# Two transformer blocks on one core: buffers shifted by 128 bytes, the inverse's turns as products on own blocks, one scan, output stored tile by tile

## The chip, the core and the metric

The kernel runs as one program on 1 core of one Trainium2 chip. The metric is the time of one execution on the device, in microseconds (us). The engines are TensorE (PE; its weight loads are PEld), VectorE (DVE), ScalarE (ACT), GpSimd (POOL) and SyncE (SP), which here only issues DMAs. Each engine runs its own instructions strictly in program order; semaphores are the only links between engines.

## The reference

The input x has 512 tokens of 1024 features. The first block is attention (a sparse NSA branch and an MLA branch, gated and summed), then an MLP with 4096 hidden features and a squared relu. The second block is a mixer of two branches, then such an MLP again, then a final norm:

```python
def second_block(x, ...):
    h = _rmsnorm(x, norm_mix_g[l])
    proj = h @ w_in[l]                       # r, k, v (1024 each), GLU (2048), gates (2048)
    ...
    a_out = _rwkv7_mixer(h, r, k, v, ...)    # 16 heads of 64, see below
    c_out = _conformer_conv_mixer(glu_in, conv_w[l], ...)   # 31 taps over time, per feature
    merged = gates[:, :, 0] * (a_out @ w_rwkv_proj[l]) + gates[:, :, 1] * (c_out @ w_conv_proj[l])
    x = x + merged @ w_out[l]
    h2 = _rmsnorm(x, norm_ff_g[l])
    x = x + jnp.square(jax.nn.relu(h2 @ w_ff1[l])) @ w_ff2[l]
    return _rmsnorm(x, norm_final_g)

    # the recurrence in _rwkv7_mixer, per head, state S (64 x 64):
    # S_t = S_{t-1} diag(w_t) + (S_{t-1} (-kk_t)) (kk_t * a_t)^T + v_t k_t^T ;  o_t = S_t r_t
```

Everything is float32.

## The kernel before

**Layout.** Features lie on the 128 partitions, 8 tiles of 128 features (`KT`), and the 512 tokens along the free dimension. A big product (helper `three`, L765 to L767) takes its weights in two parts, `whi` and `wlo`, and its activations in two parts as well (`ah`, `oh`, `yh`, `coh`, `aoh`, `hidden`), all in the type fp32r: per 128 x 128 block of weights three matmuls of 512 columns, hi by hi, hi by lo, lo by hi. ACT makes `whi` (L1295) and POOL `wlo` (L680) from the weight block that SP has loaded into `raw`. Everything else on PE is plain fp32. In nearly all products the weights are stationary and the activations are the moving operand; in the product of `uv` (L768 to L770) `cqh` is stationary and `whi` moves.

**Buffers.** They lie in SBUF in the order in which they are declared. In the built program the start addresses within a partition are: `whi` 54016, `wlo` 62208, `ah` 70400, all multiples of 256. After the small `rs`, `mod` and `modg` the rest begins at 117888, which is 128 more than a multiple of 256: `oh`, `coh` and the first `hidden` are there, and `cqh`, `yh`, `aoh` and the second `hidden` at 150656, also 128 over. `x` is at 16512, 128 over as well, and `tmp` at 103168, a multiple of 256.

**Stages.** Attention and its output (to about 560 us), MLP 1 (to about 960), the mixer of block 2 with the loop described next (to about 1713), its projections `pr`, `pc`, `wo2` (to about 1870), MLP 2, and the final norm. An MLP takes the hidden features in 4 chunks of 1024; per chunk 8 products that read `ah` and 8 that read `hidden`.

**The mixer's loop.** `rwkv_order()` returns one list of named steps, and every engine walks it and issues its share: that list is each engine's order. It has 8 tiles j of two heads (`hh` 0 and 1), each in chunks of 64 tokens. The recurrence is solved chunk by chunk with products: `mb` and `mk` make the masked matrices (`ma`, `mr`, `ka`, `kr`), then a 64 x 64 triangular matrix is inverted in `LEVELS` = 5 doubling levels. A level `lv` is: `ip` (PE: `ma` by the turned inverse `ix`, L1167; DVE masks it out of PSUM, L2153), `iy` (PE: `ip` by `iy`, L1172; DVE adds it to the inverse `iy`, L2161), and, but for the last level, `inv` (PE turns `iy`, L1156; ACT copies it into `ix`, L1334). Each is done for both heads. `iy` and `ix` hold both 64 x 64 blocks of a 128-token tile with zeros beside them, so 128 columns for each of the 4 token tiles. The first level's `iy0` is made by DVE (head 0) and POOL (head 1). After the levels come `tav` (L1178), `rr` (L1184, DVE L2170), `opa` (L1202), `pt`, `qq`, six state steps `st` (PE L1226, DVE L2182 and L2185) one after another, and `ost`. `opv` (L1195) stands ahead of the levels.

**What fills the waits.** Between these dependent steps stands work of the next tile. `tile_ahead(j + 1)` lists it: parts of the r, k, v and GLU products (two 128 x 128 blocks, 6 matmuls, each) and the steps that hang on them (`scan`, a running sum of 64 tokens, eight of them, L2071; `mix`, L2026; `kk`, L2083 to L2088; `kkss`, L2093, ending in a reciprocal, L2095, that waits for ACT's square root). `slot(taps)` puts one part and its steps, and then `taps` taps of the 31-tap convolution, which are one DVE instruction each (L2005). There are 14 slots of 2 taps inside the levels, 2 of 1 tap behind `tav` and `rr`, and the last tap comes ahead of the next tile's convolution input (L2124). The products of ("glu", j + 1, 0) lie between the state steps as filler for PE, one block each; the last tile has no such product.

**PSUM.** Banks are handed out in turn by `bank_places`; PE waits for the bank's reader before it fills one again.

## Time and profile before

| | us |
|---|---|
| median of 3 runs (lowest, highest) | 2248.98 (2247.29, 2251.56) |
| the profiled execution, its own time | 2251.5 |
| its span, first to last instruction | 2249.7 |
| PE busy | 2103.1 (93% of the span) |
| DVE, ACT, POOL busy | 1188.6, 800.9, 736.3 |
| mean granted clock of TensorE | 0.971 of 2.4 GHz |

How to read the rows further down. A row of windows has: the stretch (us from the span's start), its length, busy us and instructions of PE, PEld, DVE, ACT and POOL, the granted clock of TensorE (1.00 is 2.4 GHz), the DMA engines' busy share, GB/s. A row of the timeline has: start (us), length (us), engine, line, operation, output and inputs, shape, how many instructions were merged, and in brackets how long the engine had been idle and what ended it. Matmuls are pipelined and their ends are modelled, so what one costs is read from start to start; a plain fp32 matmul is two instructions in the trace, a turn (`transpose`) one. A row of one tile's instructions has the count, the shortest, median and longest duration in ns, the first and last start in us, and shapes. A row of waits has the total us, how many, and the longest. DVE instructions that read two operands from SBUF while POOL works can take much longer than their median.

### The profile page before, as it was taken

Reading aid. Unit: us, or ns where it says so; the run is one execution under the profiler, and the core shown is the slowest. Engines: PE = TensorE matmul, PEld = TensorE weight load, DVE = VectorE, ACT = ScalarE, POOL = GpSimd, SP = SyncE. Lnnn points to the kernel's source line nnn. Section 1 sums busy time; section 2 is a strip of 40 time slices with the busy share of each in tenths; the row PEclk is TensorE's granted clock in tenths of the full one; section 3 lists DMA queues with packets and bytes.
Section 4 is the critical chain, followed back from the end, with each engine's and each line's share of the span. In section 5 each row is a group of like instructions: output and inputs, shape, how many; then the busy total and the mean of one; then the engine's idle time right before and its main releaser. Section 6 shows DMA issues by size and latency. Waiting matters only on the chain. (4 is left out here: it accounts for less than half of the span.)

```text
span 2249.7 us, 34219 instructions
## 1 busy us (share of the span) xinstructions
PE 2103.1 (93%) x13936; PEld 1650.2 (73%) x13936; DVE 1188.6 (53%) x1963; ACT 800.9 (36%) x1292; POOL 736.3 (33%) x347
## 2 busy tenths in 40 slices
PE   6898989999999999988999999999999998999997
PEld 5775567887788888766777776676777787888885
DVE  6427775333652342738778668777813456523322
ACT  2336655223332232443333333333333434322321
POOL 0221021444344444542232133223223443444442
PEclk9989999999899999999999999999999999999998
DMA  7531011533232333231101111101122322233331
GB/s 263 187 128 38 30 47 66 175 116 95 70 98 94 94 96 97 82 106 41 34 32 46 34 34 45 43 29 44 44 85 98 122 94 76 93 94 98 99 95 57
DMA packets 51450, 186.51 MB, mean 83 GB/s; under 512 B 5728, under 2 KB 6880, under 8 KB 50784
## 3 DMA queue, kind: packets, MB, share of 16 engines
q1 hardware_dynamic: 47520, 174.49, 23.8%
q10 hardware_dynamic: 3776, 9.83, 1.2%
q8 instruction: 113, 1.85, 0.4%
q14 instruction: 41, 0.34, 0.0%
HBM read 178.01 MB, written 6.29 MB: 82 GB/s over the span
## 5 line engine op out<-in xcount | busy, mean ns | idle before, releaser
L680 POOL TENSOR_TENSOR wlo<-raw,whi 128x1024 fp32r<-128x1024 f32 x266 | 644.5, 2424 | 1337.8 <-ACT whi L1295 1337.7
L765 PE MATMUL psum<-ah,whi 128*128 128x512 f32 x1288 | 538.2, 418 | 26.5 <-POOL wlo L680 16.0
L766 PE MATMUL psum<-ah,whi 128*128 128x512 f32 x1288 | 512.0, 398 | 0.0
L767 PE MATMUL psum<-ah,wlo 128*128 128x512 f32 x1288 | 511.6, 397 | 0.0
L1295 ACT ACTIVATE whi<-raw 128x1024 fp32r<-128x1024 f32 x266 | 280.2, 1054 | 367.2 <-PE psum L767 304.0
L765 PEld LDWEIGHTS psum<-ah,whi 128*128 128x128 f32 x1288 | 247.5, 192 | 98.2 <-POOL wlo L680 26.1
L767 PEld LDWEIGHTS psum<-ah,wlo 128*128 128x128 f32 x1288 | 247.2, 192 | 54.3
L766 PEld LDWEIGHTS psum<-ah,whi 128*128 128x128 f32 x1288 | 248.3, 193 | 43.5 <-issue 0.2
L2005 DVE SCALAR_TENSOR_TENSOR x<-upad,vec,x 128x512 f32<-128x512 f32 x240 | 211.5, 881 | 5.2
L765 PE MATMUL psum<-hidden,whi 128*128 128x512 f32 x536 | 213.0, 397 | 0.0
L766 PE MATMUL psum<-hidden,whi 128*128 128x512 f32 x536 | 212.7, 397 | 0.0
L767 PE MATMUL psum<-hidden,wlo 128*128 128x512 f32 x536 | 212.6, 397 | 0.0
L1716 DVE SCALAR_TENSOR_TENSOR hidden<-tmp,hidden 128x512 fp32r<-128x512 f32 x72 | 154.0, 2139 | 49.0 <-ACT hidden L1330 49.0
L765 PEld LDWEIGHTS psum<-hidden,whi 128*128 128x128 f32 x536 | 101.3, 189 | 24.5
L767 PEld LDWEIGHTS psum<-hidden,wlo 128*128 128x128 f32 x536 | 101.2, 189 | 24.5
L766 PEld LDWEIGHTS psum<-hidden,whi 128*128 128x128 f32 x536 | 101.2, 189 | 24.4
L1334 ACT ACTIVATE sq<-psum 128x512 f32<-128x512 f32 (+2 forms) x88 | 49.1, 572 | 195.9 <-PE psum L767 195.2
L1942 DVE TENSOR_TENSOR tmp<-sq 128x512 f32<-128x512 f32 x64 | 48.6, 759 | 105.6 <-ACT sq L1334 102.2
L1950 DVE TENSOR_TENSOR x<-psum,x 128x512 f32<-128x512 f32 x32 | 22.1, 692 | 142.2 <-PE psum L767 142.2
L1952 DVE SCALAR_TENSOR_TENSOR x<-psum,mod,x 128x512 f32<-128x512 f32 x32 | 24.0, 749 | 116.4 <-PE psum L767 116.3
L1334 ACT ACTIVATE ix<-psum 128x512 f32<-128x512 f32 x80 | 45.9, 597 | 75.4 <-PE psum L1156 74.6
L1427 ACT ACTIVATE sm<-sm,stat 128x128 f32<-128x128 f32 (+3 forms) x96 | 53.2, 555 | 42.4 <-DVE stat L1857 42.0
(340 smaller groups left out, 2916.8 us busy)
## 6 DMA issues: line engine op xcount, KB each, us to landing
raw<-in_w SPq DMA_DIRECT2D x322, 512.0 KB, 3.5
x<-in_x SPq DMA_DIRECT2D x1, 2048.0 KB, 7.9
x_kept<-x ACTq DMA_DIRECT2D x1, 2048.0 KB, 9.7
ao_kept<-ao ACTq DMA_DIRECT2D x8, 256.0 KB, 2.0
aof<-ao_kept ACTq DMA_DIRECT2D x1, 2048.0 KB, 10.8
x<-x_kept ACTq DMA_DIRECT2D x1, 2048.0 KB, 8.4
out<-x SPq DMA_DIRECT2D x1, 2048.0 KB, 6.3
lwt<-in_lw ACTq DMA_DIRECT2D x8, 128.0 KB, 2.0
```

Of the source, the lines that this page charges most:

```text
L680: pool.tensor_tensor(wlo[:, s % NHL, :], raw_of(SPLITS[s]), whi[:, s % NHL, :].bitcast(F32), ALU.subtract).then_inc(lo_done, 1)
L765: pe.matmul(dst, wh, h_, start=first, stop=False)
L766: pe.matmul(dst, wh, l_, start=False, stop=False)
L767: return pe.matmul(dst, wl, h_, start=False, stop=last)
L1295: act.activation(whi[:, s % NHL, :], raw_of(SPLITS[s]), ACT.Copy).then_inc(hi_done, 1)
L1334: emptied_by(act.activation(dst, bank(name) if src is None else src, kw.pop("func", ACT.Copy), **kw), name)
L1427: act.activation(probs[:, u % PROBS[tag], 0:w], probs[:, u % PROBS[tag], 0:w], ACT.Exp, bias=st[:, u % PROBS[tag], 0:1], scale=-1.0, accum ...
L1716: dve.scalar_tensor_tensor(dst_lo, tmp[:, n % NTMP, :], bias, dst_hi.bitcast(F32), ALU.add, ALU.subtract).then_inc(hl_ready, 1)
L1942: dve.tensor_tensor(slot(("hid", n, c, m)), sq[:, e % 2, :], sq[:, e % 2, :], ALU.mult).then_inc(pre_split, 1)
L1950: emptied_by(dve.tensor_tensor(x[:, m, :], bank(what), x[:, m, :], ALU.add), what)
L1952: emptied_by(dve.scalar_tensor_tensor(x[:, m, :], bank(what), gate(m), x[:, m, :], ALU.mult, ALU.add), what)
L2005: ins = dve.scalar_tensor_tensor(acc, src, tap, acc, ALU.mult, ALU.add)
```

## The change

- A buffer `to_line` of 128 bytes that nothing uses is declared behind `modg`. All buffers behind it that are not in the mixer loop's own group move up by 128 bytes: `oh`, `coh`, `hidden` to 118016, `cqh`, `yh`, `aoh`, `hidden` to 150784, all now multiples of 256. In the loop's group sizes change too, and `ma` to `st` go from multiples of 256 to 128 over.
- `ix` and `iy` hold only their own blocks, 64 columns for each token tile. `inv` turns each block by a product with a 64 x 64 part of the unit matrix (16 matmuls of 64 x 64 for two heads, where there were 8 turns of 128 x 128). The additions on DVE and POOL and ACT's copies have 256 columns instead of 512.
- `rr`, `opv` and `opa` do both heads in one step, head 0 and head 1 in turn for each token tile; `rr` needs one PSUM bank and one DVE instruction of 128 partitions instead of two of 64.
- The masking of `mr` and `kr` is one DVE instruction instead of four. The eight scans are one scan of 512 columns that multiplies its running sum by a mask (`later`, 512 more columns in `rw`) which is 0 at a chunk's start.
- The reciprocals behind ACT's square roots become steps of their own, `kkinv` and `gninv`, that stand later in the list.
- The taps are spread by a table `TAPS`, with 3 behind `qq` and one behind every second state step.
- The output is stored by 8 DMAs of 256 KB, each behind its own tile of the final norm, where one DMA of 2 MB was behind the last.

```diff
+TAPS = (1, 2, 2, 2, 2, 1, 2, 2, 2, 0, 2, 1, 1, 2, 2, 1)
...
-            + v[2:3] + [("lg2", j)] + v[3:] + [("kkss", j)] + g[:1] + [("mix", j, 2)] + g[1:2] + [("kkb", j)] + g[2:3] + [("bonus", j)]
+            + v[2:3] + [("lg2", j)] + v[3:] + [("kkss", j)] + g[:1] + [("mix", j, 2), ("kkinv", j)] + g[1:2] + [("kkb", j)] + g[2:3] + [("bonus", j)]
...
-        out += [("akv", j, 0), ("akv", j, 1), ("inv", j, 1, 0), ("opv", j, 0), ("opv", j, 1)]
+        out += [("akv", j, 0), ("akv", j, 1), ("inv", j, 1, 0), ("opv", j)]
+        if j:
+            out.append(("gninv", j - 1))
...
-        out += [("tav", j, 0), ("tav", j, 1)] + slot(1) + [("rr", j, 0), ("rr", j, 1)] + slot(1)
-        out += [("opa", j, 0), ("opa", j, 1)] + last[:1] + [("pt", j, 0), ("pt", j, 1)] + last[1:2] + [("qq", j, 0), ("qq", j, 1)]
+        out += [("tav", j, 0), ("tav", j, 1)] + slot() + [("rr", j)] + slot()
+        out += [("opa", j)] + last[:1] + [("pt", j, 0), ("pt", j, 1)] + last[1:2] + [("qq", j, 0), ("qq", j, 1), ("conv", j, 3)]
...
-            out += [("st", j, c)] + last[1 + c:2 + c]
+            out += [("st", j, c), ("conv", j, (c + 1) % 2)] + last[1 + c:2 + c]
...
+        sb("to_line", [P, 32])
...
-            ix, iy, ip = both("ix", TT * P), both("iy", TT * P), both("ip", TT * CH)
+            ix, iy, ip = both("ix", TT * CH), both("iy", TT * CH), both("ip", TT * CH)
...
-            sp.wait_ge(xn_ready, 2 * KT)
-            sp.dma_start(out.rearrange("p (k s) -> p k s", k=KT), x[:, :, :]).then_inc(stored, 16)
-            sp.wait_ge(stored, 16)
+            for k in range(KT):
+                sp.wait_ge(xn_ready, KT + k + 1)
+                sp.dma_start(out[:, k * S:k * S + S], x[:, k, :]).then_inc(stored, 16)
+            sp.wait_ge(stored, 16 * KT)
...
-                    for t in range(TT):
-                        mm = pe.transpose(b[:, t * P:t * P + P], iy[hh][:, t, :], eye)
+                    for t, own in own_chunks:
+                        dst, src = b[own, t * CH:t * CH + CH], iy[hh][own, t, :]
+                        mm = pe.matmul(dst, src, eye[own, own], start=True, stop=True)
...
-                    hh = f[2]
-                    wait_emptied(pe, ("tav", j, hh))
+                    for hh in range(2):
+                        wait_emptied(pe, ("tav", j, hh))
                     for t in range(TT):
-                        mm = pe.matmul(b[RN * hh:RN * hh + RN, t * P:t * P + P], tav[:, t, 0, hh, :], mr[hh][:, t, :],
-                                       start=True, stop=True)
+                        for hh in range(2):
+                            mm = pe.matmul(b[RN * hh:RN * hh + RN, t * P:t * P + P], tav[:, t, 0, hh, :], mr[hh][:, t, :],
+                                           start=True, stop=True)
...
-                    for c in range(NCK):
-                        cols = slice(c * CH, c * CH + CH)
-                        last = dve.tensor_tensor_scan(cw[:, cols], ones[:, 0:CH], sw[:, cols], 0.0, ALU.mult, ALU.add)
...
+                    last = dve.tensor_tensor_scan(cw[:, :], later, sw[:, :], 0.0, ALU.mult, ALU.add)
...
+                elif kind == "kkinv":
                     dve.wait_ge(kkroot_done, j + 1)
                     dve.reciprocal(nrt[:, :], nrt[:, :]).then_inc(nrm_ready, 1)
```

PE ahead of the levels of tile 6, before (in names of `order` rows the head is the last digit of a buffer; xN merges equal rows):

```order
L1156 MATMUL psum<-eye_ones,iy0 128x128 x4
L1243 MATMUL psum<-rw,sq 128x2 x4
L1162 MATMUL psum<-vtk,ka0 64x64 x8
L1162 MATMUL psum<-vtk,ka1 64x64 x8
L1156 MATMUL psum<-eye_ones,iy1 128x128 x4
L1195 MATMUL psum<-kr0,vtk 64x128 x4
L1195 MATMUL psum<-kr1,vtk 64x128 x4
L1167 MATMUL psum<-ix0,ma0 64x64 x8
```

The same place now:

```order
L1164 MATMUL psum<-eye_ones,iy0 64x64 x8
L1253 MATMUL psum<-rw,sq 128x2 x4
L1170 MATMUL psum<-vtk,ka0 64x64 x8
L1170 MATMUL psum<-vtk,ka1 64x64 x8
L1164 MATMUL psum<-eye_ones,iy1 64x64 x8
L1205 MATMUL psum<-kr0,vtk 64x128
L1205 MATMUL psum<-kr1,vtk 64x128
L1205 MATMUL psum<-kr0,vtk 64x128
L1205 MATMUL psum<-kr1,vtk 64x128
```

Four turns of 128 x 128 per head became eight products of 64 x 64, and the eight products of `opv` now change the head each time; the order of the steps is the same.

DVE around the scan, between the additions of level 2 and the masking of level 3 in a middle tile, before:

```order
L2161 TENSOR_TENSOR iy<-psum,iy 128x512 x2
L2005 SCALAR_TENSOR_TENSOR x<-upad,vec,x 128x512 x2
L2026 SCALAR_TENSOR_TENSOR rkv<-psum,omu,rkvp 128x512
L2071 SCALAR_TENSOR_TENSOR cw<-eye_ones,sw 128x64 x8
L2005 SCALAR_TENSOR_TENSOR x<-upad,vec,x 128x512 x2
L2153 TENSOR_TENSOR ip<-psum,rw 128x256 x2
```

Now:

```order
L2161 TENSOR_TENSOR iy<-psum,iy 128x256 x2
L2015 SCALAR_TENSOR_TENSOR x<-upad,vec,x 128x512 x2
L2036 SCALAR_TENSOR_TENSOR rkv<-psum,omu,rkvp 128x512
L2079 SCALAR_TENSOR_TENSOR cw<-rw,sw 128x512
L2015 SCALAR_TENSOR_TENSOR x<-upad,vec,x 128x512
L2153 TENSOR_TENSOR ip<-psum,rw 128x256 x2
```

One scan stands where eight were, and one tap is gone from behind it.

DVE from the masking of level 4 to that of level 5, before:

```order
L2153 TENSOR_TENSOR ip<-psum,rw 128x256 x2
L2026 SCALAR_TENSOR_TENSOR rkv<-psum,omu,rkvp 128x512
L2083 TENSOR_SCALAR kk<-rkv,vec 128x512
L2084 TENSOR_SCALAR tmp<-rate,vec 128x512
L2086 SCALAR_TENSOR_TENSOR rkv<-tmp,rkv 128x512
L2088 SCALAR_TENSOR_TENSOR tmp<-rkv,vec 128x512
L2005 SCALAR_TENSOR_TENSOR x<-upad,vec,x 128x512 x2
L2161 TENSOR_TENSOR iy<-psum,iy 128x512 x2
L2005 SCALAR_TENSOR_TENSOR x<-upad,vec,x 128x512 x2
L2093 TENSOR_SCALAR nrt<-psum 128x8
L2095 RECIPROCAL nrt<-nrt 128x8
L2005 SCALAR_TENSOR_TENSOR x<-upad,vec,x 128x512 x2
```

Now:

```order
L2153 TENSOR_TENSOR ip<-psum,rw 128x256 x2
L2036 SCALAR_TENSOR_TENSOR rkv<-psum,omu,rkvp 128x512
L2088 TENSOR_SCALAR kk<-rkv,vec 128x512
L2089 TENSOR_SCALAR tmp<-rate,vec 128x512
L2091 SCALAR_TENSOR_TENSOR rkv<-tmp,rkv 128x512
L2093 SCALAR_TENSOR_TENSOR tmp<-rkv,vec 128x512
L2161 TENSOR_TENSOR iy<-psum,iy 128x256 x2
L2015 SCALAR_TENSOR_TENSOR x<-upad,vec,x 128x512 x2
L2098 TENSOR_SCALAR nrt<-psum 128x8
L2015 SCALAR_TENSOR_TENSOR x<-upad,vec,x 128x512
L2153 TENSOR_TENSOR ip<-psum,rw 128x256 x2
L2036 SCALAR_TENSOR_TENSOR rkv<-psum,omu,rkvp 128x512
```

Two taps behind `kk` and one behind `kkss` are gone, and the reciprocal stands behind the masking of level 5 and the next `mix`.

## Rows read from the trace of the kernel before

**Rows 1.** Windows: a middle tile of the mixer's loop, a longer one, the last one.

```profile
1494.42:1574.99 80.57, 75.58 (x882) 56.80 (x879) 60.78 (x118) 29.30 (x44) 22.75 (x13) 1.00 0.12 37
1169.12:1251.22 82.10, 77.12 (x882) 58.10 (x878) 60.77 (x118) 29.52 (x44) 22.74 (x13) 0.98 0.13 38
1574.99:1648.08 73.09, 69.00 (x850) 54.66 (x846) 51.70 (x95) 22.24 (x35) 15.11 (x7) 0.98 0.14 41
```

**Rows 2.** Timeline of PE in MLP 1, two matmuls reading `hidden`, two reading `ah`.

```profile
690.39 0.40 PE L765 MATMUL psum<-hidden,whi 128*128 128x512 f32 x1
...
705.09 0.39 PE L765 MATMUL psum<-hidden,whi 128*128 128x512 f32 x1
...
706.48 0.39 PE L765 MATMUL psum<-ah,whi 128*128 128x512 f32 x1
...
711.92 0.39 PE L765 MATMUL psum<-ah,whi 128*128 128x512 f32 x1
```

**Rows 3.** Instructions of one tile: fp32r (`ah`, `oh`, `cqh`), plain fp32 (`x`, `tmp`).

```profile
L765 PE MATMUL psum<-ah,whi x1288: 387/390/798, 44.7 to 2140.2; 128*128 128x512 f32 x184
...
L765 PE MATMUL psum<-oh,whi x64: 390/394/501, 465.1 to 511.9; 128*128 128x512 f32 x64
...
L768 PE MATMUL psum<-whi,cqh x8: 390/394/497, 318.1 to 323.6; 128*128 128x512 f32 x8
...
L1249 PE MATMUL psum<-x,eye_ones x16: 591/592/593, 1713.5 to 1720.0; 128*128 128x512 f32 x16
...
L1129 PE MATMUL psum<-tmp,rw x16: 589/591/595, 1004.5 to 1556.7; 128*128 128x512 f32 x16
```

**Rows 4.** Waits of PE in the middle tile of rows 1, then in the last.

```profile
PE psum L1172 <- DVE ip L2153: 2.7, 2, 1.6
PE psum L1156 <- DVE iy L2161: 1.2, 2, 1.1
...
PE psum L1226 <- DVE st L2185: 2.4, 5, 0.5
```

**Rows 5.** Timeline of PE in the loop: turns, 64 x 64 products, `rr`, the `gnb` spread.

```profile
1451.63 1.09 PE L1156 MATMUL psum<-eye_ones,iy 128*128 128x128 f32 x8
1452.48 0.48 PE L765 MATMUL psum<-ah,whi 128*128 128x512 f32 x1
...
1454.05 1.15 PE L1167 MATMUL psum<-ix,ma 64*64 64x64 f32 x32
1455.13 0.50 PE L765 MATMUL psum<-ah,whi 128*128 128x512 f32 x1
...
1476.66 1.58 PE L1184 MATMUL psum<-mr,tav 128*64 128x128 f32 x16
...
1507.48 1.09 PE L1125 MATMUL psum<-eye_ones,gnt 128*64 128x128 f32 x16
```

**Rows 6.** Timeline of DVE in the middle tile: the scan, taps, evictions, the reciprocal.

```profile
1523.48 2.96 DVE L2071 TENSOR_TENSOR_SCAN cw<-eye_ones,sw 128x64 f32<-128x64 f32 x8
1526.37 1.51 DVE L2005 SCALAR_TENSOR_TENSOR x<-upad,vec,x 128x512 f32<-128x512 f32 x2
1527.91 0.76 DVE L2153 TENSOR_TENSOR ip<-psum,rw 128x256 f32<-128x256 f32 x2
...
1530.14 1.29 DVE L2161 TENSOR_TENSOR iy<-psum,iy 128x512 f32<-128x512 f32 x2
...
1546.89 0.20 DVE L2095 RECIPROCAL nrt<-nrt 128x8 f32<-128x8 f32 x1 [1.29 <-ACT nrt L1599]
```

**Rows 7.** Timeline at the end, then DMA issues (KB each, us to landing).

```profile
2237.66 5.35 DVE L1976 SCALAR_TENSOR_TENSOR x<-x,vec,psum 128x512 f32<-128x512 f32 x8 [2.23 <-PE psum L840]
...
x_kept<-x ACTq DMA_DIRECT2D x1, 2048.0 KB, 9.7
ao_kept<-ao ACTq DMA_DIRECT2D x8, 256.0 KB, 2.0
...
out<-x SPq DMA_DIRECT2D x1, 2048.0 KB, 6.3
```

More of the change, by code:

```diff
@@ L405, in rwkv_constants @@
     own = lambda m: np.where(i < CH, m[:, :CH], m[:, CH:])
-    out = [own(i < t), same & (i <= t)]
+    out = [own(i < t), same & (i <= t), np.broadcast_to(np.arange(S) % CH > 0, (P, S))]
     for lv in range(LEVELS + 1):
@@ L542, in build_program @@
         usig, og, tf = tmp[:, 0, :], tmp[:, 1, :], tmp[:, 2, :]
-        strict, incl = rw[:, 0:CH], rw[:, CH:CH + P]
-        level = [rw[:, CH * (3 + lv):CH * (4 + lv)] for lv in range(LEVELS + 1)]
-        own_eye = rw[:, CH * (4 + LEVELS):CH * (5 + LEVELS)]
-        heads = rw[:, CH * (5 + LEVELS):CH * (5 + LEVELS) + P]
+        strict, incl, later = rw[:, 0:CH], rw[:, CH:CH + P], rw[:, CH + P:CH + P + S]
+        rest = rw[:, CH + P + S:]
+        level = [rest[:, CH * lv:CH * (lv + 1)] for lv in range(LEVELS + 1)]
+        own_eye = rest[:, CH * (1 + LEVELS):CH * (2 + LEVELS)]
+        heads = rest[:, CH * (2 + LEVELS):CH * (2 + LEVELS) + P]
         with ExitStack() as at:
```

82 lines of the change are left out of this document (35 added, 47 removed).

## The prediction

> **What bounds the kernel now.** I read the page first: PE is busy 93% of the span, the next engine 53%. So a change is worth what it takes from PE's own work, plus what it takes from the places where PE stands still. I then cut the mixer's loop into its tiles with the windows [rows 1]. A middle tile lasts 80.57 us, PE is busy for 75.58 of them, so it stands still for 5.0; DVE is busy for 60.8, 75%, and is no bound on average. The waits of PE in that tile [rows 4] say on whom: 2.7 us on DVE's masking in `ip`, 1.2 us on DVE's additions in `iy`; the other 1.1 us are on ACT. The last tile waits differently: 2.4 us are the state steps, each of which waits for DVE. The timeline of DVE [rows 6] shows why PE waits: DVE is in order and comes to its mask late, with a scan of 2.96 us and taps of 0.75 us each ahead of it. In the MLPs PE does not wait at all; there only the pace of the matmuls counts [rows 2].
>
> **Shift by 128 bytes.** In the MLP, 63 matmuls on `hidden` go by from 690.39 to 705.09, 233.3 ns each; 24 on `ah` from 706.48 to 711.92, 226.7 ns each [rows 2]. Same weights, same shape, clock 1.00; the visible difference is the address of the moving operand: `ah` starts at a multiple of 256, `hidden` 128 over. The other buffers at 128 over look like `hidden`: `oh` has a median of 394 ns where `ah` has 390, and so has `cqh` as the stationary operand [rows 3]. Afterwards all of them start at multiples of 256. I take 226.7 for all. `hidden`: 2 MLPs x 4 chunks x 64 blocks x 3, and 72 more ahead of MLP 2, are 1608 matmuls x 6.6 ns = 10.6 us. The other five buffers have 888 matmuls; by the medians the difference is 4, by the start times of `hidden` it is 6.6, I take 5.5: 4.9 us. PE hides behind nothing in these stages, except that in `pc` the next weights are only just ready; I take off 0.5. **Minus 15.0 us**, from 0 (the address is not the cause) to 16.5.
>
> **PE's own work in the loop.** Eight turns take 0.85 us from start to next start, 32 instructions of 64 x 64 products 1.08 [rows 5]. The new `inv` has exactly the latter's shape: +0.23 for each of 4 pairs, and for the first level's two single ones, which are a pair apart, about +0.07 each: +1.06 us in a tile. Against it stand `opv`, `rr`, `opa`: 16 instructions in 1.58 us with four products of one head and then four of the other, where the spread of `gnt`, 128 x 64 by 128 columns as well, but with the head changing each time, takes 1.09 [rows 5]. Three times -0.49 is -1.47. Sum -0.4 us per tile, **minus 3.3 us** in 8 tiles. The bounds are +1.06 x 8 = +8.5 (changing heads brings nothing) and -1.47 x 8 = -11.8 (the turns cost no more than before).
>
> Here a rule speaks against the change. The rows show that products into the two halves of the partitions, in turn, run partly side by side: 1.09 against 1.58 us. The Trainium skill (TensorE: Matmul & The Clock Gate, The mechanism) says that a weight load overlaps with running matmuls "only when row_grp differs", and here all use all 128 rows. By that rule the term of the three products would be 0 and the sum 11.8 us higher; the row of `gnt` does not agree with it, and I go by the row.
>
> **PE's waits in the loop.** The two rows of waits [rows 4] hold four in a middle tile, 1.6 and 1.1, 1.1 and 0.1 us; the timeline places them. (1) 1.6 us ahead of `iy` of level 3, behind the scan: DVE now has one tap less (0.75), two additions of 256 columns, which should cost what the two masks cost, 0.76 against 1.29 [rows 6], and one scan for eight. The trace has no scan of 512 columns. It can't cost less than one 512-column addition, 0.65, nor more than the eight, 2.96; a 64-column piece takes 0.37, and I take twice the addition, 1.4. That is 0.75 + 0.53 + 1.5 = 2.8 us less against a wait of 1.6; at the upper bound of the scan 0.3 us would be left. (2) 1.1 us ahead of `inv` of level 4, behind `kk`: two taps less and smaller additions, 2.0 us. (3) 1.1 us ahead of `iy` of level 5, behind `kkss`: DVE stood 1.29 us for ACT's root ahead of the reciprocal [rows 6], which moves behind the next mask, and a tap less: over 2 us. (4) 0.1 us in level 1: a tap less. So all 3.9 us should go. `gninv` moves past no DVE instruction and brings nothing. The taps reappear where DVE was idle: three behind `qq`, where it waits for ACT's copy, and three between the state steps, where PE has one block of filler, 3 x 0.23 us and what lies around it, for every step. DVE's load falls by about 6.4 us to 54.4, 72% of a tile, so it stays no bound. ACT's 1.1 us: about half hang on DVE's norm step, which now comes about 1 us earlier (smaller `iy0`, merged masks), and go; the wait ahead of the first state step stays. Something new will appear when PE comes earlier: taps stretched by POOL's reads, PSUM banks that now turn differently. I allow 0.6. So 3.9 + 0.5 - 0.6 = 3.8 us per tile, bounds 0 and 4.4, in 7 tiles: **minus 26.6 us**. A middle tile: 80.57 - 0.4 - 3.8 = 76.4 us.
>
> The last tile has no filler between its state steps. Two of the three taps there stand ahead of a step that PE waits for: a tap of 0.75 less DVE's slack of about 0.3, twice, +0.9; of its other waits (73.09 - 69.00 - 2.4 = 1.7 us [rows 1, 4]) I let 0.6 go, by the same cuts as above. **Plus 0.3 us.**
>
> **The output.** The last tile of x is ready at 2237.66 + 5.35 = 2243.0, and the 2 MB land 6.3 us later [rows 7]. Now seven of the eight parts are on their way by then. 256 KB take 2.0 us in `ao_kept` [rows 7], the tiles come every 0.67 us. If the parts keep up, the gain is 6.3 - 2.0 = 4.3; at the rate of `x_kept`, 9.7 us for all of it from the first tile on (2238.4), it is 1.2. **Minus 4.0 us**; the write of `out` itself is faster than `x_kept`.
>
> **Nothing from the rest.** `rw` is 256 KB larger, loaded behind MLP 1 once, well ahead of its first use.
>
> **The sum.** -15.0 - 3.3 - 26.6 + 0.3 - 4.0 = -48.6 us on the profiled execution's 2251.5: 2202.9. That execution lies 2.5 above the median of 2248.98, so the forecast for the median is **2200.4 us**, 2.2% faster.
>
> **Rivals.**
> - *The shift brings nothing*: the slow pace belongs to something else of these buffers, for instance to where in memory they are. Against it: they lie at two far places and are equally slow. 2215.4. 10%.
> - *DVE keeps the waits*: PE comes 4 us earlier and finds DVE late elsewhere. For it: POOL's reads stretch single taps, and DVE is in order. Against: at 72% load there is room. Half of the waits stay: 2213.7; nearly all: 2225. 13%.
> - *The small buffers pay*: `ma` to `st` go from multiples of 256 to 128 over. If their 740 small instructions per tile paid 3.3 ns each, it would be 2.4 us per tile, 2220. Against it: plain fp32 has 592 ns with `x`, 128 over, and 591 with `tmp` at a multiple of 256 [rows 3]. 5%.
> - *Slower, by TensorE's clock*: now the loop runs at 1.00, but a tile at 0.98 costs 1.5 us more [rows 1], which is 0.02 x 80. If the loop, with other shapes and gaps on PE, were granted less of the time the upper level, 2.4 GHz, each 0.01 would cost 0.8 us per tile. From a mean of 0.92 in all 8 tiles on the 49 us are used up; at 0.90 it gives about 2264. Nothing in the loop points to it, and gaps get fewer. 3%.
> - *More than forecast*: no new waits, turns at no extra cost, clock dips gone: 2192. Inside the first case's range.
>
> **How the numbers follow.** The forecast as worked out 69%, the rivals 10, 13, 5 and 3. The range takes the first case's own width (no new waits, the whole shift and output: -8 and more; a few tenths per tile more: +8) and reaches to the shift's failure and to the small buffers': 2188 to 2221. Faster by over 0.2%, about what the measurement can tell: 0.96; within it: 0.01; slower: 0.03.
>
> **What would show it.** `hidden` at 227 ns from start to start and medians of 390 for all fp32r buffers; middle tiles of 76.4 us, with no wait of PE on `ip` or `iy` above 0.3; `inv` pairs at 1.08 and `opv`, `rr`, `opa` at 1.09; a scan near 1.4 us; the end 2 us behind the last tile of x. I am wrong if `hidden` stays at 233, or if a middle tile is above 78.

## The result

| | before | after |
|---|---|---|
| median us (lowest, highest) | 2250.27 (2247.29, 2253.56) | 2226.34 (2218.32, 2229.22) |
| profiled execution, its span | 2251.5, 2249.7 | 2225.8, 2224.0 |
| mean granted clock of TensorE | 0.971 | 0.961 |

The ratio is 0.9888, 95% interval 0.9858 to 0.9917: 1.1% faster, where 2.2% were forecast. 2226.3 lies above the range of 2188 to 2221. The sign was right, the size was not, and the mean clock has fallen.

**The expected parts came.** The timeline of PE in MLP 1 after the change (columns as in the rows of before):

```profile
684.96 0.39 PE L772 MATMUL psum<-hidden,whi 128*128 128x512 f32 x1
...
704.90 0.39 PE L773 MATMUL psum<-hidden,whi 128*128 128x512 f32 x1
```

Between the two starts lie 88 matmuls, 19.94 us, so 226.6 ns each; it was 233.3 [rows 2]. The instructions that read `oh`, by line, now have a median of 389 where there was 394 [rows 3]:

```profile
L772 PE MATMUL psum<-oh,whi x64: 389/389/504, 467.4 to 513.7; 128*128 128x512 f32 x64
```

The timeline of PE in one middle tile of the loop, a pair of turns and `rr`:

```profile
1368.29 1.15 PE L1164 MATMUL psum<-eye_ones,iy 64*64 64x64 f32 x32
1369.37 0.50 PE L772 MATMUL psum<-ah,whi 128*128 128x512 f32 x1
...
1382.43 1.09 PE L1193 MATMUL psum<-mr,tav 128*64 128x128 f32 x16
1383.46 0.50 PE L772 MATMUL psum<-ah,whi 128*128 128x512 f32 x1
```

The turns take 1.08 us and `rr` 1.03, as forecast from [rows 5]. And the waits of PE in the tile from 1324.05 to 1405.04 are these (us in total, times, longest):

```profile
PE psum L1237 <- DVE st L2182: 1.6, 1, 1.6
PE psum L1237 <- ACT qs L1625: 0.6, 1, 0.6
PE psum L1253 <- ACT ktok L1344: 0.2, 1, 0.2
```

The 3.9 us on `ip` and `iy` [rows 4] are gone. In their place stands one wait of 1.58 us, on the state step `st`.

**The tiles did not get as short as that.** The windows of the eight tiles:

```profile
1004.99:1086.57 81.58, 78.98 (x973) 59.22 (x973) 56.58 (x91) 24.08 (x39) 23.61 (x14) 0.90 0.12 35
1086.57:1164.78 78.21, 75.91 (x1002) 56.81 (x999) 58.42 (x98) 27.36 (x44) 22.46 (x13) 0.98 0.13 41
1164.78:1244.44 79.66, 77.35 (x1003) 57.63 (x999) 58.57 (x98) 27.36 (x44) 22.45 (x13) 0.96 0.14 40
1244.44:1324.05 79.61, 77.30 (x1003) 57.55 (x999) 58.24 (x97) 27.18 (x44) 22.46 (x13) 0.96 0.14 40
1324.05:1405.04 80.99, 78.68 (x1002) 58.36 (x999) 58.58 (x98) 27.36 (x44) 22.46 (x13) 0.94 0.14 39
1405.04:1484.68 79.64, 77.34 (x1003) 57.52 (x999) 60.17 (x97) 27.36 (x44) 22.03 (x13) 0.96 0.13 38
1484.68:1564.13 79.45, 77.14 (x1002) 57.56 (x999) 58.52 (x98) 27.36 (x44) 22.46 (x13) 0.96 0.12 38
1564.13:1636.20 72.07, 68.01 (x969) 53.92 (x966) 45.35 (x83) 20.40 (x35) 14.15 (x7) 0.98 0.14 42
```

A middle tile has 78.2 to 81.0 us where 76.4 were forecast. PE stands still for 2.3 us of it (length less busy; before 5.0 [rows 1]), but it is *busy* for 75.9 to 78.7 us, where before it was 75.6: the same or less work takes longer, and the tile with the lowest clock is the longest. The clock is 0.94 to 0.98 where it was 0.98 to 1.00. Three short windows in the tile from 1324.05 on show where it falls:

```profile
1391.30:1393.90 2.60, 1.22 (x7) 0.70 (x7) 2.49 (x4) 0.00 (x0) 0.76 (x1) 1.00 0.70 202
1393.90:1404.10 10.20, 9.97 (x37) 5.68 (x37) 4.89 (x14) 0.00 (x0) 0.00 (x0) 0.50 0.00 0
1404.20:1410.00 5.80, 5.80 (x78) 4.53 (x78) 3.31 (x7) 1.77 (x3) 0.53 (x1) 1.00 0.01 3
```

From 1391.3 to 1393.9 PE, at 2.4 GHz, works for only 1.2 of 2.6 us; the next 10.2 us are granted 0.50, which is 1.2 GHz; then 2.4 again. Such a stretch of 3.4 to 10.2 us begins in this gap or at most 2.1 us behind it in each of the first seven tiles. By the record of the granted clock, 61 us of the loop now go by at 1.2 GHz, where before it was 13. Ten of the 61 stand at the loop's start, behind PE's wait of 2.27 us for the first `arow`; the kernel before has that wait too, but no such stretch behind it in its trace. A stretch of 3.41 us costs 1.4 to 1.5 us (79.66 against 78.21 above, 82.10 against 80.57 in [rows 1]), so 48 us more cost some 20 to 21.

**Why PE stands still there** the timeline of that tile shows:

```profile
1388.11 2.36 POOL L689 TENSOR_TENSOR wlo<-raw,whi 128x1024 fp32r<-128x1024 f32 x1 [4.70 <-ACT whi L1305]
...
1388.43 4.97 DVE L2015 SCALAR_TENSOR_TENSOR x<-upad,vec,x 128x512 f32<-128x512 f32 x3
...
1390.43 1.63 POOL L739 TENSOR_TENSOR arow<-rkv,ewall 128x512 f32<-128x512 f32 x1
...
1391.33 0.33 PE L1237 MATMUL psum<-qs,pts 64*64 64x64 f32 x4 [0.57 <-ACT qs L1625]
...
1393.44 0.28 DVE L2179 SCALAR_TENSOR_TENSOR su<-qs,wc 128x64 f32<-128x64 f32 x1
1393.76 0.23 DVE L2182 TENSOR_TENSOR st<-psum,su 128x64 f32<-128x64 f32 x1
...
1394.13 0.48 PE L1237 MATMUL psum<-st,pts 64*64 64x64 f32 x4 [1.58 <-DVE st L2182]
```

The three taps behind `qq` take 4.97 us, not 3 x 0.75 = 2.3. Meanwhile POOL makes `wlo` and then its half of `arow`. `qs` is ACT's copy of the result of `qq`; from it and the last state DVE makes `su`, and it adds the product of the state step to that, which gives the next `st`. `qs` is ready at 1391.2, DVE comes to `su` only at 1393.44, and PE waits for `st`.

My first theory, W in the first expectations, was: POOL's reads stretch the taps (this half is G further on), so PE waits 1.6 us, and for that idle time TensorE's clock falls (this half is I). Rivals: the clock falls for the new shapes or their order (P), and three taps are too many with or without POOL (T).

### The profile page after: what moved, and what is told of

It is laid out like the page before. It is cut to its first block, busy times and chain, and to the rows that moved or that the text cites. A ratio compares the mean times of both kernels' runs of the same rounds, so it can differ in the third digit from the quotient of the medians.

```text
span 2224.0 us, 35984 instructions
## 1 busy us (share of the span) xinstructions
PE 2098.7 (94%) x14896; PEld 1651.4 (74%) x14896; DVE 1167.5 (52%) x1803; ACT 785.5 (35%) x1292; POOL 733.2 (33%) x347
## 4 chain that ended last, share of the span: by engine, by line
PE 80%; DVE 9%; ACT 3%; issue 3%; POOL 2%; DMA 2%; DVEq 0%; SPq 0%; ACTq 0%; POOLq 0%
PE psum L772 21%; PE psum L773 19%; PE psum L774 19%; PE psum L1180 2%; PE psum L1175 2%; POOL wlo L689 2%; DVE x L2015 2%; PE psum L1164 2%; PE psum L909 2%; DMA raw<-in_w 1%; PE psum L930 1%; DVE sq_sum L1712 1%; PE psum L915 1%; PE psum L1122 1%; PE psum L1154 1%
## 5 line engine op out<-in xcount | busy, mean ns | idle before, releaser
L772 PE MATMUL psum<-ah,whi 128*128 128x512 f32 x1288 | 545.1, 423 | 27.5 <-POOL wlo L689 16.7
L773 PE MATMUL psum<-ah,whi 128*128 128x512 f32 x1288 | 517.4, 402 | 0.0
L774 PE MATMUL psum<-ah,wlo 128*128 128x512 f32 x1288 | 516.8, 401 | 0.0
L2015 DVE SCALAR_TENSOR_TENSOR x<-upad,vec,x 128x512 f32<-128x512 f32 x240 | 225.0, 938 | 5.2
L772 PE MATMUL psum<-hidden,whi 128*128 128x512 f32 x536 | 209.7, 391 | 0.1
L773 PE MATMUL psum<-hidden,whi 128*128 128x512 f32 x536 | 209.1, 390 | 0.0
L1164 PEld LDWEIGHTS psum<-eye_ones,iy 64*64 64x64 f32 x1280 | 43.7, 134 | 17.1 <-issue 17.1
```

The costliest lines, as they stand in the source:

```text
L772: pe.matmul(dst, wh, h_, start=first, stop=False)
L773: pe.matmul(dst, wh, l_, start=False, stop=False)
L774: return pe.matmul(dst, wl, h_, start=False, stop=last)
L1164: mm = pe.matmul(dst, src, eye[own, own], start=True, stop=True)
L2015: ins = dve.scalar_tensor_tensor(acc, src, tap, acc, ALU.mult, ALU.add)
```

## Experiments

Each run was timed beside the kernel before on the same chip; the ratio is to that.

**Taps moved away.** The kernel after, with

```diff
-... + [("qq", j, 0), ("qq", j, 1), ("conv", j, 3)]
+... + [("qq", j, 0), ("qq", j, 1)]
-        out += [("akv", j, 0), ("akv", j, 1), ("inv", j, 1, 0), ("opv", j)]
+        out += [("akv", j, 0), ("akv", j, 1), ("inv", j, 1, 0), ("opv", j), ("conv", j, 1)]
         if j:
             out.append(("gninv", j - 1))
+        out.append(("conv", j, 2))
```

> The changed kernel with the three taps behind qq moved ahead of level 1 (one behind gnv, two behind gninv), where VectorE was idle. Theory W (the taps behind qq meet GpSimd's reads, take 5 us, TensorE waits 1.6 us for the first state step and its clock falls in that gap): the wait of L1237 on VectorE goes, the half-clock stretch at each tile's end goes or gets rare, a middle tile takes 76.3 to 77 us instead of 78.2 to 81, and the time is about 2203 us. Theory P (the clock falls because of the new shapes, the 64x64 turns or the heads in turn): the wait goes (-1.6 us in 7 tiles, -11 us) but the granted clock stays at 0.94 to 0.98 in every tile: about 2215 us.

Measured: 2195.8 us, ratio 0.9747 (0.9725 to 0.9769). The windows of its first tile and a middle one:

```profile
1004.46:1078.04 73.58, 71.98 (x972) 54.10 (x972) 53.94 (x91) 23.97 (x39) 23.18 (x14) 1.00 0.13 39
1228.40:1303.58 75.18, 74.46 (x1002) 56.12 (x998) 55.71 (x98) 27.18 (x44) 22.00 (x13) 1.00 0.14 42
```

The first seven tiles all have clock 1.00, with every new shape in them, and in a middle one PE stands still for 0.7 us. So P falls in this form, and three DVE instructions of 0.75 us, in the wrong place, cost 30 us. Some 4 of these, in the two profiled executions, belong to the stretch at the loop's start, which this trace does not have. The mean clock of the four timed executions says the same as the traces, 0.969 to 0.973 here and 0.958 to 0.966 in the kernel after. The time is 7 us below what W had said, and a middle tile 1.2 us below the 76.4 of the prediction.

**Shift alone.** The kernel before with

```diff
+        sb("to_line", [P, 32])
```

> The kernel before with the 128-byte buffer alone. If the address of the operands sets the pace: all fp32r matmuls at 227 ns from start to start instead of 233, time 15 us less, ratio 0.9933. If the trace of the changed kernel got its 227 ns from something else in the change: no difference. All buffers of the mixer loop move by 128 bytes as well here; if that cost something, the loop's tiles would be longer than 80.57 us.

Measured: 2234.98 us, 0.9932 (0.9910 to 0.9953), which is -15.3 us with an interval from -20 to -11. The term of -15.0 holds. In its trace 106 matmuls on `hidden` from 675.77 to 699.79 go by every 226.6 ns. Its middle tiles take 80.63 us where they took 80.57, so that the small buffers, which move here too, cost next to nothing.

**The new spread alone.** The kernel before with the table `TAPS`, the three taps behind `qq` and those between the state steps:

```diff
-            return got + [("conv", j, taps)]
+            return got + [("conv", j, taps.pop(0))]
-... + [("qq", j, 0), ("qq", j, 1)]
+... + [("qq", j, 0), ("qq", j, 1), ("conv", j, 3)]
-            out += [("st", j, c)] + last[1 + c:2 + c]
+            out += [("st", j, c), ("conv", j, (c + 1) % 2)] + last[1 + c:2 + c]
```

> The kernel before with the new spread of the taps alone (table, 3 behind qq, one behind every second state step). Theory W: the waits on ip and iy get smaller (about 3 of 3.9 us per tile), a wait of about 1.6 us appears ahead of the second state step, and the granted clock falls near the end of most tiles, so the time is within 10 us of before, 2245 to 2255. Theory P: the same new wait but the clock stays at 1.00 in the middle tiles, as before; tiles of about 79 us, time about 2238.

Measured: 2236.96 us, 0.9933 (0.9906 to 0.9959). It came out as the rival P said. A middle tile:

```profile
1166.55:1244.68 78.13, 74.89 (x881) 56.96 (x878) 63.32 (x118) 28.98 (x44) 23.45 (x13) 1.00 0.13 40
```

and its waits, by PE's own:

```profile
PE psum L1177 <- DVE ip L2158: 1.1, 2, 0.8
PE psum L1231 <- DVE st L2190: 1.1, 1, 1.1
```

The wait on `st` is there, so G's half came; but it has 1.1 us where W said 1.6, and a stretch at 1.2 GHz follows it in only one of the seven tiles, the first. Two other tiles have a stretch of 3.4 us elsewhere, 1.2 us behind a wait of 0.49 us that stands among the small products ahead of the levels. So either the new shapes have a share in what happens behind the wait on `st`, or 1.1 us are too little. The next run has the new shapes and such a wait.

**Heads apart.** The kernel after, with head 0 and then head 1 in `opv`, `rr` and `opa`:

```diff
-                    for t in range(TT):
-                        for hh in range(2):
+                    for hh in range(2):
+                        for t in range(TT):
```

> The changed kernel with the four products of head 0 and then the four of head 1 in opv, rr and opa. Each of the three takes 1.51 us instead of 1.02, 1.5 us more per tile at full clock. Theory W: the half-clock stretches stay, time 8 to 12 us above the changed kernel's 2226. Theory P with the heads in turn as the cause: the stretches go, tiles near 78.5, time at or below 2226.

Measured: 2238.24 us, 0.9947 (0.9916 to 0.9978). The timeline of PE shows `rr` as it was before the change:

```profile
1135.73 1.58 PE L1193 MATMUL psum<-mr,tav 128*64 128x128 f32 x16
```

A tile at clock 1.00 has 76.0 us of busy PE against 74.5 with the heads in turn: 1.55 us for three groups, 0.52 each (forecast 0.49). Its windows, a tile with and one without the fall of the clock:

```profile
1076.87:1154.67 77.80, 76.01 (x1002) 57.61 (x999) 57.92 (x98) 27.36 (x44) 22.46 (x13) 1.00 0.14 41
1318.67:1400.63 81.96, 80.16 (x1003) 59.84 (x999) 57.92 (x97) 27.37 (x44) 22.45 (x13) 0.94 0.13 39
```

The stretches did not go and the time is 12 us above the kernel after, as W said; P with the heads in turn as the cause falls. But the ten executions lie far apart, from 2221.7 to 2252.8 us at mean clocks from 0.967 to 0.953, and the trace is of one of the faster. Here the wait on `st` is 1.07 us as in the spread alone, and in five of the seven tiles 10.2 us at 1.2 GHz follow. So the length of this wait alone doesn't set the price, and what stands around it, the new shapes too, has a share.

**The gap filled.** This one takes the idle time of PE away and leaves DVE as late as it is. In `st` with c == 2:

```diff
+                        if c == 2 and j < KT - 1:
+                            for _ in range(3):
+                                pe.matmul(b, eye, mr[0].rearrange("p t n -> p (t n)"), start=True, stop=True)
                         wait_emptied(pe, ("st", j, c - 1))
```

> The kernel after, with three more 128x512 products of plain fp32 in each of the first seven tiles, on TensorE, ahead of its wait for the second state step. Their result is overwritten by the state step's own products, so the output is the same. They take 3 x 0.59 = 1.8 us, as long as the 1.58 us for which TensorE now stands still there. VectorE, GpSimd and everything else keep their work. Theory I (the idle stretch is what lowers TensorE's clock): the wait goes, the half-clock stretches behind it go too, a middle tile becomes 76.2 + 0.7 + 0.2, about 77.0 us instead of 79.4 to 81.0, and the kernel takes about 2206 us although it does more work. Rival S (the clock falls for the many small products ahead of it, or for the load of the whole tile, not for the idle time): the half-clock stretches stay at 6.8 us a tile, the tile grows by 0.2, and the kernel takes 2227 to 2229 us.

Measured: 2216.99 us, 0.9845 (0.9831 to 0.9858). The windows of a middle tile, and of the place of the gap and the 10 us behind it:

```profile
1399.00:1476.74 77.74, 77.02 (x1008) 57.25 (x1004) 60.34 (x98) 27.33 (x44) 22.04 (x13) 1.00 0.12 39
```

```profile
1389.50:1392.30 2.80, 2.80 (x10) 1.04 (x9) 1.84 (x5) 0.00 (x0) 0.00 (x0) 1.00 0.35 140
1392.30:1402.50 10.20, 10.20 (x105) 7.07 (x105) 6.41 (x16) 1.77 (x3) 0.00 (x0) 1.00 0.01 2
```

No middle tile has a stretch at 1.2 GHz any more, and a kernel with 2.6 us more work per tile is 9 us faster. That is I's result and not S's. The time is 11 us above what I expected. About 5 of them come from the price of the filler: I took the length of a row (0.59 us) for the price of a product, but a plain fp32 one is two instructions, 0.43 us apart, so the three took 2.57 us, and 75.18 + 2.57 = 77.75 is the tile, where I had said 77.0. Most of the rest lies outside the loop, where this profiled execution took 4.4 us more than that of the kernel after, with 8 us more at 1.2 GHz.

**POOL later.** The kernel after, with POOL's work held back until DVE has done the first `su`:

```diff
                 if kind == "part" and f[2] == 0:
+                    if f[1][0] == "glu" and f[1][1] and f[1][2] == 0:
+                        pool.wait_ge(u_ready, (NCK - 2) * (f[1][1] - 1) + 1)
                     weights_ahead(SPLIT_AT[f[1]] + 1)
```

> The kernel after, with one more wait on GpSimd: its split of the glu block's weights (2.36 us) and the product into arow behind it (1.63 us) start only when VectorE has done the sum ahead of the first state step, so behind the three taps behind qq instead of beside them. The three taps stay where they are. Theory G (the taps are long because GpSimd reads SBUF beside them): three taps take 2.3 us instead of 4.97, VectorE is ready before ScalarE's copy of qq, TensorE's wait of 1.58 us and the half-clock stretches go, middle tiles take about 75.3 us and the kernel 2196 to 2200 us. Rival T (three taps are too many in themselves, or something else than GpSimd stretches them): the taps stay near 5 us and the kernel within 3 us of 2226. Second rival: GpSimd's work, now some 3 us later, is late for TensorE's weights, with a wait of 1 to 2 us a tile on wlo: 2205 to 2212 us.

Measured: 2211.82 us, 0.9822 (0.9800 to 0.9844). That is the range of the second rival, but not for its reason: in a middle tile PE has no wait on `wlo`. The timeline:

```profile
1386.09 2.32 DVE L2017 SCALAR_TENSOR_TENSOR x<-upad,vec,x 128x512 f32<-128x512 f32 x3
...
1389.04 0.28 DVE L2181 SCALAR_TENSOR_TENSOR su<-qs,wc 128x64 f32<-128x64 f32 x1 [0.63 <-ACT qs L1627]
...
1389.40 2.38 POOL L689 TENSOR_TENSOR wlo<-raw,whi 128x1024 fp32r<-128x1024 f32 x1 [8.34 <-DVE su L2181]
1389.42 0.23 DVE L2184 TENSOR_TENSOR st<-psum,su 128x64 f32<-128x64 f32 x1
...
1389.68 2.18 DVE L2181 SCALAR_TENSOR_TENSOR su<-st,wc,qs 128x64 f32<-128x64 f32 x1
...
1392.27 0.33 PE L1239 MATMUL psum<-st,pts 64*64 64x64 f32 x4 [0.91 <-DVE st L2184]
...
1394.19 0.33 PE L1239 MATMUL psum<-st,pts 64*64 64x64 f32 x4 [0.70 <-DVE st L2184]
```

Without POOL beside them the three taps take 2.32 us, and DVE even waits for ACT: G holds, T falls. But now POOL's split meets the second `su`, which takes 2.18 us in place of 0.28 and ends when the split does. PE waits as long as before, 0.91 + 0.70 us, in two pieces. Of the first seven tiles four have a stretch of 3.4 us at their end, one has 6.8 and two have none, where the kernel after has 3.4 to 10.2 in all; most middle tiles take 78.3 us. Moving what collides only chose another victim; the moved taps had left slack for it.

The addition into `st` at 1389.42, with one operand from PSUM, was not stretched beside the same split; the `su` 0.26 us later, with `st` and `qs` from SBUF, was. By the Trainium skill (SBUF — State Buffer, Who interferes with whom) a VectorE instruction with two SBUF inputs contends with a GpSimd instruction that reads SBUF, and whoever starts second is blocked until the other ends; the two rows agree with it.

**The output alone.** The kernel before with eight stores in place of one:

> The kernel before, with the output's store alone made as in the change: eight stores, each behind its tile of x. By the two traces the span ended 6.7 us behind the last tile of x in the kernel before and 3.2 us behind it in the kernel after. If that is the stores' own effect: 3.5 us less, ratio 0.9984, and nothing else moves. Rival (the end behind the last tile is set by the store's fixed time, and eight stores only add to it): ratio 1.000.

Measured: 2248.37 us, 0.9988 (0.9977 to 0.9999), -2.7 us with an interval from -5 to 0. The interval reaches almost to the rival's 1.000, so the time alone hardly tells the two apart; the traces do. In the timeline of the kernel after the last tile of x is done at 2215.48 + 5.36 = 2220.8, and the span ends at 2224.0, so 3.2 us later, where it was 6.7 in the kernel before [rows 7]; in this run's own trace it is 3.1. By that, -3.5; forecast -4.0.

```profile
2215.48 5.36 DVE L1986 SCALAR_TENSOR_TENSOR x<-x,vec,psum 128x512 f32<-128x512 f32 x8 [2.23 <-PE psum L847]
```

The DMA's row (KB each, us to landing):

```profile
out<-x SPq DMA_DIRECT2D x8, 256.0 KB, 2.5
```

**Is it any idle time?** In the middle tiles of the kernel before PE waits 1.6 us ahead of `iy` of level 3 and its clock holds behind that. So I made such a wait there, with the new shapes. The kernel after with

```diff
-TAPS = (1, 2, 2, 2, 2, 1, 2, 2, 2, 0, 2, 1, 1, 2, 2, 1)
+TAPS = (1, 2, 2, 3, 2, 3, 2, 2, 2, 0, 2, 1, 1, 2, 2, 1)
-... + [("qq", j, 0), ("qq", j, 1), ("conv", j, 3)]
+... + [("qq", j, 0), ("qq", j, 1)]
```

> The kernel after, but the three taps from behind qq stand elsewhere: one in a place of level 2 where VectorE has room, two behind the turn of level 2, ahead of the mask of level 3, where VectorE has no slack in e1_tail_moved (mask done at 1335.28, TensorE's iy at 1335.24). So TensorE should stand still for about 1.5 us a tile ahead of iy of level 3, the place where it waited 1.6 us in the kernel before, instead of behind qq. Theory A (any stretch of about 1.6 us without work lowers the clock): half-clock stretches of about 6.8 us behind it in most tiles, middle tiles near 79.5 us, the kernel 2222 to 2230 us. Rival B (where it stands matters: behind qq there are only small products and single steps around the wait, here there are whole groups of full-width products on both sides, as in the kernel before, whose loop kept its clock): no half-clock stretches in most tiles, middle tiles 75.2 + 1.5 = 76.7 us, the kernel 2205 to 2209 us.

Measured: 2205.94 us, 0.9802 (0.9770 to 0.9834). The windows of a middle tile and of the 10 us behind the wait, then the wait in the timeline:

```profile
1233.32:1309.98 76.66, 74.54 (x1002) 56.14 (x998) 56.02 (x98) 27.18 (x44) 22.03 (x13) 1.00 0.14 41
```

```profile
1268.00:1278.00 10.00, 10.00 (x122) 7.23 (x121) 7.83 (x16) 5.13 (x8) 2.38 (x1) 1.00 0.18 48
```

```profile
1266.43 1.15 PE L1180 MATMUL psum<-iy,ip 64*64 64x64 f32 x32 [1.39 <-DVE ip L2153]
```

The rival B: a wait of 1.39 us a tile costs 1.5 us (76.66 against 75.18), and no middle tile loses its clock; nor does the first, whose wait there is 1.73 us. The idle time behind `qq` costs its 1.6 us and up to 4.2 more by the clock. There PE had waited 0.57 us shortly before, and between the two waits it had one state step and one short step of the next tile; here full groups stand on both sides. So I holds only together with the place; and the new shapes, which are all in this kernel, do not lower the clock by themselves.

The length counts in this place too. In the first tile of the kernel before, the wait ahead of `iy` of level 3, again between full groups, is longer, and 3.4 us at 1.2 GHz begin 1.1 us behind it:

```profile
1040.50 1.15 PE L1172 MATMUL psum<-iy,ip 64*64 64x64 f32 x32 [2.23 <-DVE ip L2153]
```

The first tiles of the shift alone and of the output alone, with 2.23 and 2.25 us, show the same; the 18 waits of 1.6 us there, in the middle tiles of these three traces, have no stretch right behind them.

**A step moved to cover the 0.57 us.** Two runs move one step of the `glu` product from between `pt` and `qq` to behind `qq`. On top of the moved taps, and with no taps between the state steps of the last tile:

```diff
-... + [("pt", j, 0), ("pt", j, 1)] + last[1:2] + [("qq", j, 0), ("qq", j, 1)]
+... + [("pt", j, 0), ("pt", j, 1), ("qq", j, 0), ("qq", j, 1)] + last[1:2]
-            out += [("st", j, c), ("conv", j, (c + 1) % 2)] + last[1 + c:2 + c]
+            out += [("st", j, c), ("conv", j, (c + 1) % 2 if j + 1 < KT else 0)] + last[1 + c:2 + c]
```

> The kernel with the three taps moved from behind qq (as in e1_tail_moved), and two changes more: the step of the glu product that stood between pt and qq now stands behind qq, where TensorE waited 0.57 us for ScalarE's copy of qs; and the last tile has no taps between its state steps, they follow later. Expected: the 0.57 us goes in seven tiles (4.0 us), the last tile's waits on st go from 3.5 back to 2.4 us (1.1 us): middle tiles 74.6 us, 2190 to 2191 us. Rival: pt's copies on VectorE or ScalarE's copy of qs are late in another place, since qq now follows pt at once, and TensorE waits as long there: 2195 to 2196 us, or 2200 and more if the clock falls behind such a wait.

Measured: 2193.69 us, 0.9735 (0.9719 to 0.9751). And the first half of that edit alone on the kernel after, whose taps stay behind `qq`:

> The kernel after, with one step of the glu product moved from between pt and qq to behind qq; the three taps stay behind qq. In e8_qs_covered this move, on top of the moved taps, shortened a middle tile from 75.18 to 74.23 us. Theory D (here VectorE, with its long taps, sets when the second state step can run, and TensorE only waits for that): the 0.57 us on qs go, the wait on st grows by as much to about 2.1 us, the tile keeps its end, half-clock stretches stay at 6.8 us a tile or more, the kernel takes 2223 to 2230 us. Rival F (the wait on qs is a cost of its own): the tile gets 0.6 to 0.9 us shorter and the kernel takes 2219 to 2221 us.

Measured: 2222.25 us, 0.9858 (0.9840 to 0.9877). In the first a middle tile has 74.23 us, 0.95 less, and the last 70.2 instead of 72.1. But in the profiled execution the clock fell at the loop's start, where it had held in that of the moved taps, and the first tile took 2.8 us more; the time is 3 us above what I expected:

```profile
1009.77:1086.13 76.36, 75.80 (x973) 57.67 (x973) 54.42 (x91) 24.07 (x39) 23.16 (x14) 0.93 0.13 38
```

In the second the 0.57 us only joined the wait on `st`, now one of 2.53 us: where DVE is the late one, a wait on ACT ahead of it costs nothing of its own. The tile without a stretch has 76.8 us, which is what the kernel after has when one takes a stretch's 1.4 us off its 78.21; so the tile kept its end, as D says. The time, 2222.25, lies between the ranges of D and F and decides nothing. D's stretches of 6.8 us and more came in only four of the seven tiles, two had 3.4 us, and one had none in spite of its 2.53 us.

**The first tile's wait filled, and a gate product in the last tile.** The kernel of the covered 0.57 us, with ten small products ahead of PE's wait for the first `arow`:

```diff
+                    if (j, i) == (0, 0):
+                        for _ in range(10):
+                            pe.matmul(b[:, 0:P], eye, eye, start=True, stop=True)
                     if i == 0:
                         pe.wait_ge(at_ready, j + 1)
```

> The kernel e8_qs_covered, with ten 128x128 products of plain fp32 in the first tile, ahead of TensorE's wait of 2.27 us for the first arow; their result is overwritten. Three of four profiles in which that wait falls (e2, e7, e8; not e1) show 10 to 14 us at half clock right behind it, and there the first tile takes 76.4 us in e8_qs_covered where it takes 73.6 in e1_tail_moved. Theory I (idle time lowers the clock): the half-clock stretch behind it goes in every execution, the first tile takes about 72.6 us, the kernel 2188 to 2191 us, and its runs lie closer together. Rival: the clock falls there for what comes ahead of the wait, or the ten products only push the tile back: 2193 to 2196 us.

Measured: 2188.06 us, 0.9711 (0.9698 to 0.9725). The first tile:

```profile
1007.82:1080.52 72.70, 71.62 (x973) 53.84 (x973) 54.30 (x91) 23.94 (x39) 23.25 (x14) 1.00 0.13 40
```

No stretch at 1.2 GHz, 3.7 us less than the tile above, and the time is in I's range. As proof of the filler's effect it is weak: of the twelve traces without it, five have no stretch at the loop's start either. Then, on top, `("gate2", 5)` in eight parts between the state steps of the last tile:

```diff
-        last = parts(("glu", j + 1, 0), KT) if j + 1 < KT else []
+        last = parts(("glu", j + 1, 0) if j + 1 < KT else ("gate2", GATES_IN), KT)
-    gates = [f for m in range(GATES_IN, 16) for f in parts(("gate2", m), 1)]
+    gates = [f for m in range(GATES_IN + 1, 16) for f in parts(("gate2", m), 1)]
```

> The kernel e10_first_filled, and in the last tile the sixth gate product is cut into eight parts that stand between its state steps, as the glu product's parts stand in the other tiles. The last tile's state steps now wait 2.4 us for VectorE and 0.4 us on the sums behind, with half-clock stretches of 3.4 to 6.8 us. Expected: those waits go, since other work stands there, and the clock holds: 2.8 us of idle time and 1.4 to 2.8 us of clock less than e10_first_filled, about 4.5 us, so 2184 to 2187 us. Rival: the end of the loop is later for ScalarE and VectorE behind it, which the gates' tail hides, so the gain is given back at the convolution's mean: within 1 us of e10_first_filled.

Measured: 2184.56 us, 0.9690 (0.9677 to 0.9703). The last tile is 73.93 us with 73.77 of them busy, and a whole gate product in it. Its waits went, but right behind the loop PE now waits 2.67 us for POOL's `wlo`, with a stretch of 3.4 us at 1.2 GHz behind that, so a part of the gain is given back there. This is the fastest kernel of the study, some 2% below the change as it was made.

## Why the prediction was wrong

**Right: shift, output, DVE's waits in the levels, the shapes.** The shift: -15.0 against -15.3 measured alone. The output: -4.0 against -3.5 by the traces, and -2.7 (-5 to 0) by the time. The heads in turn: -0.49 per group against -0.52. In the trace of the moved taps the products of the two heads start 6 to 7 ns apart, a pair every 109 ns; head by head one product starts every 109 ns. By the rule of the Trainium skill that I had set against this term (TensorE: Matmul & The Clock Gate, The mechanism) it would have been 0; these runs do not agree with that for products whose outputs lie in the two halves of the partitions. The turns: +1.06 a tile against +0.91. PE's own work in a tile fell by 1.1 us (75.58 to 74.46), not 0.4; of the 0.6 beyond these two terms the larger part is in the steps from `mk` to `akv`, and I tested no cause for it. All 3.9 us of waits on `ip` and `iy` went.

**Wrong, the step that failed: "three behind `qq`, where it waits for ACT's copy".** I costed these taps at 0.75 us each, from a stretch in which POOL was silent, and called them hidden. Beside POOL's split and `arow` they took 4.97 us. I had named this ("taps stretched by POOL's reads") and allowed 0.6 us for all of it; it was 1.58. My rival of 13%, that DVE is late elsewhere because POOL's reads stretch single taps, had this mechanism; I had argued against it with DVE's load of 72%, a mean over the tile that says nothing of the few us behind `qq`. The trace of before had what was needed. Two rows further down its timeline of the middle tile:

```profile
1554.05 1.28 POOL L715 TENSOR_TENSOR rate<-kk,rate 128x512 f32<-128x512 f32 x1 [3.33 <-PE psum L1178]
1554.09 3.47 DVE L2005 SCALAR_TENSOR_TENSOR x<-upad,vec,x 128x512 f32<-128x512 f32 x2
...
1563.39 2.36 POOL L680 TENSOR_TENSOR wlo<-raw,whi 128x1024 fp32r<-128x1024 f32 x1 [4.92 <-ACT whi L1295]
1565.72 1.18 POOL L731 TENSOR_TENSOR arow<-rkv,ewall 128x512 f32<-128x512 f32 x1
```

Two taps beside POOL take 3.47 us where two without it take 1.51 [rows 6], and behind `qq` POOL reads for 3.5 us on end.

The term of the scan was mis-read for the same reason. In the first tile the scans meet no work of POOL; these are the eight of the kernel before, then the one of the kernel after:

```profile
1036.91 1.55 DVE L2071 TENSOR_TENSOR_SCAN cw<-eye_ones,sw 128x64 f32<-128x64 f32 x8
...
1036.44 1.22 DVE L2079 TENSOR_TENSOR_SCAN cw<-rw,sw 128x512 f32<-128x512 f32 x1
```

In the middle tiles both meet POOL's split and take 2.96 and 2.86 us. So a 64-column piece costs 0.19 us (1.55 / 8) and not 0.37, nearly half of the 2.96 was POOL, and one scan for eight saved 0.1 us there, not 1.5. The wait of 1.6 us went even so: the tap took 0.8 us off it (the spread alone), the smaller additions 0.5, and PE comes 0.2 later by its longer turns (the last two are estimates from the rows).

**Wrong, the second step: the clock's rival.** I wrote that "nothing in the loop points to it, and gaps get fewer", and gave it 3%. The gaps did get smaller, 2.3 us in place of 5.0 per tile, but what remained stood in one place, behind small products. Something did point to it: in three tiles of the kernel before 3.4 us go by at 1.2 GHz, once behind the first tile's wait of 2.23 us, twice behind a wait of only 0.49 us among the small products ahead of the levels. The rival's scale was right (0.01 of clock is 0.8 us a tile), its size was in between: mean 0.95 in the loop's first seven tiles, not below 0.92.

**The sum for the loop**, from the profiles: idle time of PE (the wait ahead of the first tile with it) 42.8 to 22.8 us, -20.0; own work -1.1 x 8 = -9; clock +20 to +21. That makes -8 to -9; the loop went from 640.3 to 631.2, -9.1. The forecast for the loop was -29.6. With the three taps moved it is 596.7, -43.6: the mechanism could give more than I forecast, and the change as made got a fifth of it. A part of that is chance: the trace of the kernel after has the stretch at the loop's start, some 4 us, and the other two do not.

**The last tile**: +0.3 forecast, 72.07 against 73.09 measured, -1.0. Its waits on `st` rose from 2.4 to 3.5 us, a little more than the +0.9 I had said; the other waits fell as much, so it stands still for 4.1 us as before, and PE's own work is 1.0 us less.

## What to carry to other kernels

Work that is laid into the idle time of one engine is costed at its length *beside what the others do there*; look in the trace at what GpSimd reads in that stretch before you put VectorE's two-input instructions there. A wait of TensorE has two prices, its length and what the clock takes behind it: look in the windows for stretches at 0.50 and at what stood ahead of them, and if a short wait can't be removed, move it between dense groups or fill it. When idle time falls in sum, ask where the rest stands.
